# Blockwise inverses of triangular chunks: a quarter of the products moved to the diagonal tiles, and the side projections moved out

## The chip, the cores and the metric

One core of a Trainium2 chip. The metric is the device time of one execution in microseconds; three runs of the kernel before are shown, and one further execution was profiled.

## The reference, cut to what matters

All tensors are float32. A first block runs two layers; in each, an RWKV-7 branch steps a 64x64 state per head over 512 tokens. A second block has a gated delta net in both directions, whose chunk form needs an inverse of a unit lower triangular 64x64 matrix per chunk, head and direction:

```
state = state*w + (state @ -kk) (kk*a)^T + v k^T; y = state @ r      # RWKV, per token, 6 heads
x = x + concat(y_a, y_b, y_c) @ w_out[i]                             # 1024 x 1024, each layer
L = where(strict, (k*beta) @ k^T * decay, 0)                         # delta net, per chunk of 64
T = triangular_solve(eye + L, eye); u = T @ vb; w = T @ (kb*exp(gc))
gate_a, gate_d = split(sigmoid(h @ w_in[gate columns]))              # 2 x 1024 columns
merged = gate_a * (attn @ w_attn_up) + gate_d * (dn @ w_dn_up)
```

The kernel brings the RWKV recurrence into chunks of 64 tokens as well, with an inverse of the same kind.

## The kernel before, in words

Activations lie with channels on the 128 partitions and 512 tokens in columns. Two heads share a tile: partitions 0 to 63 and 64 to 127, the two halves. The program is a row of phases; in a phase each engine has its own instruction list, ordered by semaphores, and a phase ends with SP clearing the semaphores and a barrier.

**`invert` (line 914)** makes all inverses of a stage at once. A stage has groups of blocks, a block being one 64x64 matrix in each half. rwkv calls it once per layer (line 1282): 4 groups of 6 blocks, one direction. `delta_net` calls it once (line 2065): 8 groups of 8 blocks, four of each direction. The inverse is built by doubling: at level 0 the 2x2 blocks are written down, and each of the five levels 1 to 5 joins blocks of 2, 4, 8, 16 and 32. It keeps the inverse `inv` and its transpose `inv_t`. A job is one group at one level, so there are 5 x groups jobs (20 and 40). A job makes `half` = lower^T-product with `inv_t` in its step (banks 2 and 3 in turn), and two steps later the products for `inv` (banks 4 and 5) and `inv_t` (banks 6 and 7); step j on TensorE thus holds the first product of job j and the second ones of job j-2. At the last level `inv` isn't made.

TensorE works on quarters of its array, named by the half it reads and the half it writes. `half` and `inv_t` go across: read in one half, written to the other. `inv` stays within its half. The order in a step is, for every block, `half`, `inv`, `inv_t`, each for both halves (lines 987 to 996). Every float32 product shows as two matmul records and two weight loads. ScalarE copies `half` out of PSUM (line 1006, one instruction for all blocks), VectorE puts `inv` (1030) and `inv_t` (1031) under the level's mask with one predicated copy each and then lets `product_used` and `t_ready` go. TensorE's step j waits for `t_ready` of job j, `half_copied` of job j-2, and `product_used` of job j-4.

Level 0: SP moves `lower` into `inv` with the halves exchanged, two transfers per group (line 960), 96 KB each in rwkv and 128 KB in delta net. TensorE transposes `lower` by the identity (line 974, shown in the trace under line 967), VectorE copies it into `inv_t` (1019), then waits for the transfers of all groups, multiplies `inv` by the mask (1022) and adds the identity (1024), and goes to the next group.

**Side work in `invert`.** After each step TensorE does `portion` of a side projection: 128x512 products of 128x128 weight tiles (line 420), each tile gathered in bank 0 or 1. In rwkv these are output tiles 4 to 7 of `w_out` on the five k-tiles of attention rows that are ready (20 products in 22 steps), which VectorE adds to x (1217). In the delta net they are four tiles of the merge's gate columns, 8 products each (32 in 42 steps), which ScalarE copies (464) and SP spills to memory (453). Output tiles 0 to 3 of `w_out` are treated so in an earlier phase (`EARLY_OUT` = 4), ten of the gate tiles before the inverse (`BEFORE_INVERSE` = 10; `SPILLED` = 14 in all).

**After the inverse.** In rwkv a loop over the 8 chunks carries the state (1297 to 1326). Then `add_projection` (1418) takes k-tiles 0 to 2 of `w_out` for all eight output tiles: 3 products each, a ring of four weight tiles loaded by SP (1431), VectorE adding each to x (1451). `merge` (2157) makes the eight tiles of `merged`: 8 products for a tile whose two gates were spilled (m below `SPILLED // 2` = 7, gates read back on line 2177), else 24, with its 1.5 MB of weights, in a ring of two; step m's load is issued when tile m-2 is done.

Of the kernel before, what the change touches and what calls it, by code (L numbers as in the profile page):

```python
# [22 lines left out]
P = 128  # L23
# [26 lines left out]
def constant_parts():  # L50
# [44 lines left out]
    parts["strict"] = wide([c < r, c > r])  # L95
    parts["strict_T"] = wide([c > r, c < r])
# [34 lines left out]
def constant_offsets():  # L131
    at, where = 0, {}
    for n, a in constant_parts().items():
        where[n] = (at, a.shape[1])
        at += a.shape[1]
    where["neg_causal"] = (where["band"][0] + P, P)
    return where, at
# [776 lines left out]
def invert(nc, M, lower, inv, inv_t, groups, gsize, dirs, side, taker):  # L914
# [7 lines left out]
    def mask(lv, flip):  # L922

        return spread_out(level[:, lv, flip:flip + dirs, :].bitcast(U32))

    def ones(lv, flip):

        return spread_out(level[:, lv, flip:flip + dirs, :])

    def spread_out(m):  # L930

        if dirs == 1:
            return m.broadcast_to([P, blocks, CH])
        return m.unsqueeze(2).broadcast_to([P, dirs, blocks // dirs, CH])

# [7 lines left out]
    with ExitStack() as stack:  # L943
# [3 lines left out]
        with phase(nc, moved=0, eyes=0, lt_ready=0, t_ready=0, masked=0, inv_ready=0, half_copied=0, made=0, product_used=0, dve=0,  # L947
                   **side.SEMAPHORES) as (block, s):
            side.attach(s)
            steps = 5 * groups + 2  # L950
            portion = lambda step: side.products * step // steps

            halves = ((0, slice(0, HD)), (HD, slice(HD, P)))
            here_there = (halves, halves[::-1])

            @block.sync
            def _(sp):
                for g in range(groups):
                    for (_, here), (_, there) in zip(*here_there):
                        sp.dma_start(inv[there, g], lower[here, g]).then_inc(s["moved"], 16)  # L960
                side.load(sp)
                sp.wait_ge(s["moved"], 32 * groups)

            @block.tensor
            def _(pe):
# [3 lines left out]
                for g in range(groups):  # L969
                    if g >= 2:  # L970
                        pe.wait_ge(s["t_ready"], g - 1)
                    for b in range(blocks):
                        for row, here in halves:
                            last = mm(bank(4 + g % 2)[here, b, :], lower[here, g, b, :], M.c("ident2")[here, :], row, row)
                    last.then_inc(s["lt_ready"], 1)
                for job in range(steps):
                    g, k, old, og = job % groups, job % 2, job - 2, (job - 2) % groups
                    if job < 5 * groups:
                        pe.wait_ge(s["t_ready"], job + 1)
                    if old >= 0:  # L980
# [6 lines left out]
                    for b in range(blocks):  # L987
                        if job < 5 * groups:
# [1746 lines left out]
```

## Time and profile before

| | us |
|---|---|
| median of 3 runs | 2558.03 (2557.32 to 2561.3) |
| profiled execution, its own time | 2548.97 |
| its span in the trace | 2547.2 |
| TensorE matmul busy | 2242.9 (88%) |
| VectorE busy | 967.8 (38%) |
| ScalarE busy | 464.3 (18%) |
| mean granted TensorE clock | 0.944 of 2.4 GHz |

In the trace PE is TensorE's matmul side, PEld its weight loads, DVE VectorE, ACT ScalarE, SPq the queue of SP. A timeline line has start, length, engine, line, operation, output<-inputs, shape, count, and in brackets the idle time before it with what ended it. The first rwkv inverse lies at 412 to 476 us of the span, the second at 1036 to 1099, the delta net's at 1648 to 1796. The second layer repeats the first.

### The profile page before, as it was taken

Reading aid. Unit: us, or ns where it says so; the run is one execution under the profiler, and the core shown is the slowest. Engines: PE = TensorE matmul, PEld = TensorE weight load, DVE = VectorE, ACT = ScalarE, POOL = GpSimd, SP = SyncE. Lnnn points to the kernel's source line nnn. Section 1 sums busy time; section 2 is a strip of 40 time slices with the busy share of each in tenths; the row PEclk is TensorE's granted clock in tenths of the full one; section 3 lists DMA queues with packets and bytes.
Section 4 is the critical chain, followed back from the end, with each engine's and each line's share of the span. In section 5 each row is a group of like instructions: output and inputs, shape, how many; then the busy total and the mean of one; then the engine's idle time right before and its main releaser. Section 6 shows DMA issues by size and latency. Waiting matters only on the chain. (4 is left out here: it accounts for less than half of the span.)

```text
span 2547.2 us, 44008 instructions
## 1 busy us (share of the span) xinstructions
PE 2242.9 (88%) x18641; PEld 1169.4 (46%) x18641; DVE 967.8 (38%) x1768; ACT 464.3 (18%) x912; POOL 230.3 (9%) x181
## 2 busy tenths in 40 slices
PE   7989978879898998887898977879879979999998
PEld 3543436634363343763444533567644444444442
DVE  1157685332026767533233551454332251111112
ACT  1021431120102142111222332412110110000000
POOL 0111300000020310000004520400000000000000
PEclk9989999989998999998999988989989989999999
DMA  4134011021315300102101001110104549999997
GB/s 158 61 141 165 9 46 36 19 83 33 104 52 188 126 18 29 36 19 91 68 17 67 34 33 54 56 47 21 39 34 140 233 174 406 421 422 422 422 422 311
DMA packets 65238, 334.92 MB, mean 131 GB/s; under 512 B 7712, under 2 KB 11296, under 8 KB 36256
## 3 DMA queue, kind: packets, MB, share of 16 engines
q1 hardware_dynamic: 65056, 332.32, 34.2%
q8 instruction: 136, 2.23, 0.4%
q14 instruction: 46, 0.38, 0.0%
HBM read 322.06 MB, written 5.77 MB: 129 GB/s over the span
## 5 line engine op out<-in xcount | busy, mean ns | idle before, releaser
L420 PE MATMUL ps<-store,side_ring 128*128 128x512 f32 x784 | 396.6, 629 | 15.9 <-DMA side_ring<-in_w_rwkv 6.6
L2419 PE MATMUL ps<-expert_ring,xe 128*64 128x512 f32 x1024 | 223.2, 593 | 2.8 <-DVE back L2528 1.7
L420 PEld LDWEIGHTS ps<-store,side_ring 128*128 128x128 f32 x784 | 136.5, 194 | 171.2 <-issue 147.7
L333 PE MATMUL ps<-store,side_ring 128*128 128x512 f32 x384 | 168.2, 601 | 1.9 <-DVE store L299 1.9
L2419 PEld LDWEIGHTS ps<-expert_ring,xe 128*64 128x64 f32 x1024 | 73.0, 137 | 149.5 <-issue 147.4
L420 PE MATMUL ps<-store 128*128 128x512 f32 x224 | 115.2, 648 | 17.4 <-DMA store<-in_w_merge 16.8
L333 PEld LDWEIGHTS ps<-store,side_ring 128*128 128x128 f32 x384 | 74.0, 193 | 94.8 <-issue 92.3
L2447 PE MATMUL ps<-expert_ring,store 128*64 128x512 f32 x512 | 111.6, 594 | 1.4 <-DVE store L2504 1.4
L1504 PE MATMUL ps<-store,weight_ring 128*128 128x512 f32 x256 | 110.7, 593 | 1.9 <-DVE store L299 1.9
L2476 ACT ACTIVATE store<-ps 128x1024 f32<-128x1024 f32 x16 | 16.4, 1024 | 417.5 <-PE ps L2419 417.5
L509 POOL TENSOR_TENSOR attn_z<-attn_z,tables 128x512 f32<-128x512 f32 (+1 forms) x24 | 37.6, 1569 | 570.3 <-PE ps L498 568.2
L2491 DVE SCALAR_TENSOR_TENSOR x<-ps,mod,x 128x512 f32<-128x512 f32 x64 | 48.1, 751 | 108.0 <-PE ps L2396 103.6
L2189 PE MATMUL ps<-store,expert_ring 128*128 128x512 f32 x160 | 71.8, 611 | 11.2 <-DMA expert_ring<-in_w_merge 11.2
L1006 ACT ACTIVATE half<-ps 128x384 f32<-128x384 f32 (+1 forms) x80 | 43.5, 544 | 204.7 <-PE ps L967 204.7
L967 PE MATMUL ps<-inverses,matrices 64*64 64x64 f32 x1280 | 76.6, 220 | 2.9 <-DVE inverses L1024 2.1
L967 PE MATMUL ps<-half,inverses 64*64 64x64 f32 x1280 | 75.9, 218 | 2.5 <-issue 2.3
L1504 PEld LDWEIGHTS ps<-store,weight_ring 128*128 128x128 f32 x256 | 48.5, 190 | 62.5 <-issue 60.9
L575 DVE COPY attn_tok<-ps 128x456 f32<-128x456 f32 x8 | 5.1, 633 | 185.6 <-PE ps L565 185.6
L967 PEld LDWEIGHTS ps<-inverses,matrices 64*64 64x64 f32 x1280 | 63.9, 135 | 24.2 <-issue 21.1
L420 PEld LDWEIGHTS ps<-store 128*128 128x128 f32 x224 | 42.4, 203 | 65.6 <-issue 44.7
L1442 PE MATMUL ps<-store,weight_ring 128*128 128x512 f32 x96 | 45.8, 640 | 30.4 <-DMA weight_ring<-in_w_out 30.4
L2447 PEld LDWEIGHTS ps<-expert_ring,store 128*64 128x64 f32 x512 | 36.1, 137 | 71.0 <-issue 68.5
(426 smaller groups left out, 3838.2 us busy)
## 6 DMA issues: line engine op xcount, KB each, us to landing
expert_ring<-in_w_expert SPq DMA_DIRECT2D x192, 1024.0 KB, 16.4
mixed<-in_w_ada SPq DMA_DIRECT2D x24, 1024.0 KB, 4.8
side_ring<-in_w_attn SPq DMA_DIRECT2D x32, 512.0 KB, 3.7
side_ring<-in_w_rwkv SPq DMA_DIRECT2D x20, 512.0 KB, 4.4
weight_ring<-in_ple_gate SPq DMA_DIRECT2D x16, 512.0 KB, 4.2
store<-in_w_merge SPq DMA_DIRECT2D x14, 512.0 KB, 3.7
side_ring<-in_w_conv SPq DMA_DIRECT2D x12, 512.0 KB, 3.5
chosen<-in_w_o SPq DMA_DIRECT2D x8, 512.0 KB, 5.7
```

The costliest lines, as they stand in the source:

```text
L333: last = nc.tensor.matmul(ps[:, u, :], ring[:, u, k, :], src[:, k, :], start=(k == 0), stop=(k == kt - 1))
L420: ins = self.nc.tensor.matmul(self.ps[:, self.banks[j % banks], :], self.ring[:, j % self.slots, k, :], self.src[:, k, :], start=(k == 0), ...
L509: self.nc.gpsimd.tensor_tensor(self.z[rows, tile, :], self.z[rows, tile, :], self.M.table(f"cos_{table}")[rows], ALU.mult).then_inc(self.s ...
L967: return nc.tensor.matmul(out, lhs, rhs, start=True, stop=True, tile_position=(row, col))
L1006: nc.scalar.activation(half[:, job % 2], bank(2 + job % 2), ACT.Copy,).then_inc(s["half_copied"], 1)
L1442: last = nc.tensor.matmul(ps[:, j % 4, :], ring[:, j % 4, k, :], src[:, k, :], start=(k == 0), stop=(k == kt - 1))
L1504: last = nc.tensor.matmul(ps[:, j % 4, :], ring[:, j % 4, k, :], h[:, k, :], start=(k == 0), stop=(k == KT - 1))
L2189: last = nc.tensor.matmul(ps[:, 4 * (m % 2) + bank, :], ring[:, m % 2, k, :], src, start=(i == 0 or parts[i - 1][0] != bank), stop=(i == 2 ...
L2419: last = nc.tensor.matmul(ps[w, 2 * ep + half, :], xe[:, ep, k, :], ring[:, unit % SLOTS, k2, S * half:S * half + S], start=(k == 0), stop ...
L2447: last = nc.tensor.matmul(ps[w, 6 + half, :], act_t[:, ep, f, :], ring[:, units[ep] % SLOTS, f2, S * half:S * half + S], start=(f == 0), s ...
L2476: nc.scalar.activation(act_in[:, ep, :], ps[:, 2 * ep:2 * ep + 2, :].rearrange("p b n -> p (b n)"), ACT.Copy).then_inc(s["in_copied"], 1)
L2491: nc.vector.scalar_tensor_tensor(out=x[:, m, :], in0=ps[:, bank, :], scalar=gain(m), in1=x[:, m, :], op0=ALU.mult, op1=ALU.add).then_inc(s ...
```

## The change

- The side projection is taken out of `invert`. Output tiles 4 to 7 of `w_out` are then made whole (8 products) in `add_projection`; tiles 0 to 3 keep 3. `SPILLED` becomes 10, so four gate tiles are made in `merge`, where m = 5 and 6 now have 24 products.
- Of the blocks of each direction the first `width * 3 // 4` stay crossed (rwkv 4 of 6, delta net 3 of 4); the others go straight for `half` and `inv_t` too, and use banks 0 and 1 for both. The transfers of level 0 exchange the halves for crossed blocks alone, in four pieces per group for two.
- TensorE's order in a step alternates straight and crossed pairs. ScalarE has two copies per job and VectorE three.
- Level 0: the copies of `inv_t` go first for all groups; `inv` becomes one predicated copy of the identity per group, as its own transfers land.
- The constants lose `strict_T`, now a part of `strict`, and gain `not_first`.

```diff
-        with phase(nc, moved=0, eyes=0, lt_ready=0, t_ready=0, masked=0, inv_ready=0, half_copied=0, made=0, product_used=0, dve=0,
-                   **side.SEMAPHORES) as (block, s):
+        with phase(nc, moved=groups, eyes=0, lt_ready=0, t_ready=0, inv_ready=0, half_copied=0, made=0, straight_used=0, product_used=0, dve=0) as (block, s):
+            side = (slice(0, HD), slice(HD, P))
+            width = blocks // dirs
+            away = width * 3 // 4
+            crossed = [b for b in range(blocks) if b % width < away]
+            straight = [b for b in range(blocks) if b % width >= away]
...
+            def in_turn(within, across):
+                order, given = [], 0
+                for i, item in enumerate(within):
+                    upto = len(across) * (i + 1) // len(within)
+                    order += [(*item, 0)] + [(*other, 1) for other in across[given:upto]]
+                    given = upto
+                return order
...
                 for g in range(groups):
-                    for (_, here), (_, there) in zip(*here_there):
-                        sp.dma_start(inv[there, g], lower[here, g]).then_inc(s["moved"], 16)
-                side.load(sp)
-                sp.wait_ge(s["moved"], 32 * groups)
+                    for r in range(2):
+                        for cross in range(2):
+                            sp.dma_start(part(inv[side[r ^ cross], g], cross), part(lower[side[r], g], cross)).then_inc(s["moved"][g], 16)
+                for g in range(groups):
+                    sp.wait_ge(s["moved"][g], 64)
...
-                        pe.wait_ge(s["half_copied"], old + 1)
+                        pe.wait_ge(s["half_copied"], 2 * old + 2)
                     if old == 0:
                         pe.wait_ge(s["t_ready"], groups)
-                        pe.wait_ge(s["inv_ready"], groups)
+                    if 0 <= old < groups:
+                        pe.wait_ge(s["inv_ready"], old + 1)
                     if old >= 2:
                         pe.wait_ge(s["product_used"], old - 1)
...
+                    within = (of("inv_t", straight) if second else []) + \
+                        (of("inv", range(blocks)) if second and old < 4 * groups else []) + (of("half", straight) if first else [])
+                    across = (of("half", crossed) if first else []) + (of("inv_t", crossed) if second else [])
+                    for what, b, cross in in_turn(within, across):
...
+                            if what == "half":
+                                last = mm(bank(2 + k if cross else k)[side[c], at, :], lower[w, g, b, :], inv_t[w, g, b, :], HD * r, HD * c)
...
                     last.then_inc(s["made"], 1)
-                    side.multiply(pe, portion(job + 1))
...
-                    nc.scalar.activation(half[:, job % 2], bank(2 + job % 2), ACT.Copy,
-                                         ).then_inc(s["half_copied"], 1)
...
+                    nc.scalar.activation(part(half[:, job % 2], 1), part(bank(2 + job % 2), 1), ACT.Copy).then_inc(s["half_copied"], 1)
+                    if job >= 2:
+                        act.wait_ge(s["straight_used"], job - 1)
+                    nc.scalar.activation(part(half[:, job % 2], 0), slots(job % 2, 0), ACT.Copy).then_inc(s["half_copied"], 1)
...
-                    dve.wait_ge(s["moved"], 32 * groups)
-                    nc.vector.tensor_tensor(view(inv[:, g]), view(inv[:, g]), ones(0, 0), ALU.mult).then_inc(s["masked"], 1)
-                    dve.wait_ge(s["masked"], g + 1)
-                    nc.vector.tensor_tensor(inv[:, g], inv[:, g], eye, ALU.add).then_inc(s["inv_ready"], 1)
+                for g in range(groups):
+                    dve.wait_ge(s["moved"][g], 64)
+                    nc.vector.copy_predicated(inv[:, g], rest, eye).then_inc(s["inv_ready"], 1)
...
+                    nc.vector.copy_predicated(part(inv_t[:, g], 0), within, slots(k, 1)).then_inc(s["straight_used"], 1)
                     if lv < 5:
                         own.mark(nc.vector.copy_predicated(view(inv[:, g]), mask(lv, 0), view(bank(4 + k))))
-                    own.step(nc.vector.copy_predicated(view(inv_t[:, g]), mask(lv, 1), view(bank(6 + k))))
+                    own.step(nc.vector.copy_predicated(part(inv_t[:, g], 1), across, part(bank(6 + k), 1)))
+                    dve.wait_ge(s["straight_used"], job + 1)
                     dve.sem_inc(s["product_used"], 1)
                     dve.sem_inc(s["t_ready"], 1)
...
-BEFORE_INVERSE, SPILLED = 10, 14
+SPILLED = 10
...
-                    added = add_projection(nc, M, lambda j: w_out(j)[:, 0:RP, :], KT, RP, y[:, 0:RP, :], x)
+                    added = add_projection(nc, M, w_out, KT, KT, y, x, short=EARLY_OUT, part=RP)
```

`add_projection` takes `part` k-tiles for j below `short` and `kt` for the others, in its loads and its products.

## Rows read from the trace of the kernel before

**Rows 1.** Busy times by window: window, length, then each engine's; clock, DMA share, GB/s.

```profile
421.50:475.80 54.30, 53.13 (x1398) 36.50 (x1394) 25.48 (x47) 9.80 (x20) 0.00 (x0) 0.98 0.04 12
1677.90:1794.00 116.10, 111.72 (x3582) 85.21 (x3582) 48.83 (x72) 24.61 (x42) 0.00 (x0) 1.00 0.06 20
1648.10:1677.90 29.80, 15.53 (x322) 13.83 (x323) 16.26 (x24) 5.52 (x10) 0.00 (x0) 0.71 0.42 107
490.00:500.00 10.00, 7.55 (x210) 6.87 (x212) 3.33 (x10) 0.66 (x2) 0.00 (x0) 1.00 0.01 3
```

**Rows 2.** Timeline of ScalarE in the inverses, one copy per step.

```profile
450.62 0.49 ACT L1006 ACTIVATE half<-ps 128x384 f32<-128x384 f32 x1 [2.11 <-PE ps L967]
452.02 0.49 ACT L1006 ACTIVATE half<-ps 128x384 f32<-128x384 f32 x1 [0.91 <-PE ps L967]
...
1686.19 0.60 ACT L1006 ACTIVATE half<-ps 128x512 f32<-128x512 f32 x1 [2.47 <-PE ps L967]
1688.06 0.60 ACT L1006 ACTIVATE half<-ps 128x512 f32<-128x512 f32 x1 [1.27 <-PE ps L967]
1691.13 0.60 ACT L1006 ACTIVATE half<-ps 128x512 f32<-128x512 f32 x1 [2.47 <-PE ps L967]
...
1783.30 0.60 ACT L1006 ACTIVATE half<-ps 128x512 f32<-128x512 f32 x1 [2.47 <-PE ps L967]
1785.17 0.60 ACT L1006 ACTIVATE half<-ps 128x512 f32<-128x512 f32 x1 [1.27 <-PE ps L967]
```

**Rows 3.** Timeline inside one block: crossed `half,inverses`, straight `inverses,half`, both halves each.

```profile
1687.03 0.23 PE L967 MATMUL ps<-half,inverses 64*64 64x64 f32 x2
1687.04 0.14 PEld L967 LDWEIGHTS ps<-inverses,half 64*64 64x64 f32 x2
1687.04 0.27 PE L967 MATMUL ps<-inverses,half 64*64 64x64 f32 x2
```

**Rows 4.** Timeline of VectorE's copies and of the TensorE work they release.

```profile
413.32 0.59 DVE L1019 COPY_PREDICATED inv_t<-consts,ps 128x384 f32<-128x384 uint32 x1 [1.81 <-PE ps L967]
414.02 0.20 PEld L967 LDWEIGHTS ps<-consts,raw 64*64 64x64 f32 x4 [0.26 <-DVEq L1020]
...
428.15 0.14 PEld L967 LDWEIGHTS ps<-inv_t,raw 64*64 64x64 f32 x2 [0.76 <-issue]
...
429.82 0.59 DVE L1030 COPY_PREDICATED inv<-consts,ps 128x384 f32<-128x384 uint32 x1 [1.56 <-PE ps L967]
430.30 0.57 DVE L1031 COPY_PREDICATED inv_t<-consts,ps 128x384 f32<-128x384 uint32 x1
...
1680.05 0.73 DVE L1030 COPY_PREDICATED inverses<-consts,ps 128x512 f32<-128x512 uint32 x1 [2.27 <-PE ps L967]
1680.67 0.71 DVE L1031 COPY_PREDICATED inverses<-consts,ps 128x512 f32<-128x512 uint32 x1
```

**Rows 5.** Timeline of SP's transfers of level 0, and VectorE's first use.

```profile
412.24 5.00 SPq L960 DMA_DIRECT2D inv<-raw  x8
418.88 0.56 DVE L1022 TENSOR_TENSOR inv<-inv,consts 128x384 f32<-128x384 f32 x1 [4.97 <-DMA inv<-raw]
...
1648.16 11.02 SPq L960 DMA_DIRECT2D inverses<-matrices  x16
```

**Rows 6.** Timeline of VectorE: the first instruction of the phase after each inverse.

```profile
477.35 0.22 DVE L1337 MEMSET state<- 128x192 f32 x1 [1.58 <-PEq L209]
...
1798.08 0.48 DVE L2123 MEMSET inverses<- 128x512 f32 x1 [4.85 <-PEq L209]
```

**Rows 7.** Two tiles of the projection on VectorE; chain of waits in the merge.

```profile
547.88 0.69 DVE L1451 TENSOR_TENSOR x<-ps,x 128x512 f32<-128x512 f32 x1 [12.57 <-PE ps L1442]
550.46 0.69 DVE L1451 TENSOR_TENSOR x<-ps,x 128x512 f32<-128x512 f32 x1 [1.88 <-PE ps L1442]
...
1943.79 7.02 DMA expert_ring<-in_w_merge
...
1950.86 20.87 PE ps L2189 x48
```

More of the change, by code:

```diff
@@ L136, in constant_offsets @@
     where["neg_causal"] = (where["band"][0] + P, P)
+    where["strict_T"] = (where["strict"][0] + CH, 2 * CH)
+    where["strict"] = (where["strict"][0], 2 * CH)
     return where, at
@@ L911, in attention_branches, with invert @@
                   M.tables.rearrange("p (u h) n -> p u h n", u=2))
-def invert(nc, M, lower, inv, inv_t, groups, gsize, dirs, side, taker):
+def invert(nc, M, lower, inv, inv_t, groups, gsize, dirs):
     ps = M.ps
@@ L922, in mask @@
     def mask(lv, flip):
[L924 to L930, printed above, removed]
+        m = level[:, lv, flip:flip + dirs, :].bitcast(U32)
         if dirs == 1:
@@ L972, in _ @@
                     for b in range(blocks):
-                        for row, here in halves:
-                            last = mm(bank(4 + g % 2)[here, b, :], lower[here, g, b, :], M.c("ident2")[here, :], row, row)
+                        for r in range(2):
+                            last = mm(bank(4 + g % 2)[side[r], b, :], lower[side[r], g, b, :], M.c("ident2")[side[r], :], HD * r, HD * r)
                     last.then_inc(s["lt_ready"], 1)
@@ new lines, in _ @@
+                    across = (of("half", crossed) if first else []) + (of("inv_t", crossed) if second else [])
+                    for what, b, cross in in_turn(within, across):
+                        at = b if cross or what == "inv" else straight.index(b) + (len(straight) if what == "inv_t" else 0)
+                        for r in range(2):
+                            c, w = r ^ cross, side[r]
+                            if what == "half":
+                                last = mm(bank(2 + k if cross else k)[side[c], at, :], lower[w, g, b, :], inv_t[w, g, b, :], HD * r, HD * c)
+                            elif what == "inv":
+                                last = mm(bank(4 + k)[w, at, :], half[w, k, b, :], inv[w, og, b, :], HD * r, HD * r)
+                            else:
+                                last = mm(bank(6 + k if cross else k)[side[c], at, :], inv[w, og, b, :], half[w, k, b, :], HD * r, HD * c)
@@ L1279, in rwkv_branch @@
             pairs_of = lambda a: a[:, :, :, :].rearrange("p (g c) j t -> p g (c j) t", c=2)
-            out_ring = sbt("side_ring", [P, 3, KT - RP, P])
-            side = SideProjection(nc, M, [add(j) for j in range(EARLY_OUT, KT)], KT - RP, y[:, RP:KT, :], out_ring, 3, (0, 1))
-            invert(nc, M, pairs_of(low), pairs_of(inv), pairs_of(inv_t), NCH // 2, 2 * RP, 1, side, "vector")
+            invert(nc, M, pairs_of(low), pairs_of(inv), pairs_of(inv_t), NCH // 2, 2 * RP, 1)
             state, xs, sa = sbt("state", [P, 2, RP, HD]), sbt("xs", [P, 2, RP, CH]), sbt("sa", [P, 2, RP, CH])
@@ L1415, in _, with add_projection @@
                     own.step(nc.vector.tensor_tensor(yr, yr, z[:, R_G:R_G + 3, :], ALU.mult))
-def add_projection(nc, M, weights, n, kt, src, x, gain=None, ready=None, free=1, ring=None):
+def add_projection(nc, M, weights, n, kt, src, x, gain=None, ready=None, free=1, ring=None, short=0, part=0):
     ps = M.ps
@@ L1438, in _ @@
                         pe.wait_ge(s["added"], j - 3)
-                    for k in range(kt):
+                    use = part if j < short else kt
+                    for k in range(use):
                         if ready and j == 0:
```

50 lines of the change are left out of this document (20 added, 30 removed).

## The prediction

> **What bounds the kernel now.** I read busy time and granted clock by stage first, because the page's totals mix stages with different limits, and then the timelines engine by engine. In the two kinds of inverse stage TensorE has the full clock (2.4 GHz) and is busy all the time, while VectorE and ScalarE are busy less than half of it [rows 1]. From one of ScalarE's copies to the next is one step of the pipeline: 1.87 us in delta net and 1.40 in rwkv for a step without a side product, 3.07 with one [rows 2]. So a side product costs 1.20 us there, more than its 0.86 in a row of its kind (part 5): nothing of it lies beside the small blocks.
>
> What is in 1.87 us? Eight blocks, each with two pairs of products across the halves (`half`, `inv_t`) and one pair within them (`inv`): 16 crossed pairs and 8 straight ones. At the last level `inv` is not made, so 16 crossed pairs alone, and the step is again 1.87, from 1783.30 to 1785.17 [rows 2]. So the crossed pairs set it, at 0.117 us each, and the straight ones are free beside them. rwkv says the same: 12 crossed pairs x 0.117 = 1.40. Inside a block, straight weight loads and matmuls start within 20 ns of crossed ones [rows 3].
>
> **The change, part by part.**
>
> 1. *Balance.* rwkv (6 blocks, 4 stay crossed): crossed 2x4 = 8 pairs, straight 2x2+6 = 10, so TensorE's work in a step, W, is 10 x 0.117 = 1.17 us for 1.40. Delta (8 blocks, 6 crossed): 12 and 12, W = 1.40 for 1.87. Last level: rwkv 0.94, delta 1.40. That both directions can be kept full no step of before shows; the bounds are these values and no gain (1.40 and 1.87). I take the full gain, since in rows 3 crossed and straight matmuls run side by side and the crossed ones, by rows 2, lose nothing by it. The Trainium skill (TensorE: Matmul & The Clock Gate, Part 3, The mechanism) says that a weight load overlaps matmuls in flight only where the row group differs; straight and crossed products of one half share it, so by that rule the balance gives nothing, which is rival A. The trace disagrees: the load at 1687.04 starts behind matmuls on both halves that started at 1687.03.
>
> 2. *What comes after W.* Step j starts when VectorE has taken job j-4, made in step j-2, for the banks are used in turn. From a step's start to VectorE's start is 429.82 - 428.15 = 1.67 us: W 1.40 and 0.27. From VectorE's end (413.91) to TensorE's start is 0.11 [rows 4]; with one more semaphore wait I take 0.14. VectorE now has three instructions for two. Start to start 384 columns are 0.48 and 512 are 0.62 [rows 4], so 128 add 0.14 and the straight part (128 columns) takes some 0.21; the last instruction counts with its whole length. rwkv: 0.21 + 0.48 + 0.44 = 1.13. Delta: 0.21 + 0.62 + 0.58 = 1.41. Two steps take W + 0.27 + this + 0.14: rwkv 2.71, a step 1.355; delta 3.22, a step 1.61. So the return through VectorE sets the step, and part of the balance is lost. The 128-column copy stands in no row: bounds 0.08, the part that doesn't grow with columns, and 0.48, as for 384; that is -0.07 to +0.14 us a step. ScalarE's two copies end before VectorE's three (its one copy of 384 columns takes 0.49, rows 2), and the `straight_used` it waits for comes from the first of these.
>
> 3. *Level 0.* All `inv_t` copies go first now, and the `inv` ones follow each landing, so steps 0 to 3 run under the transfers. But VectorE does every group's `inv` before job 0, and step 4 waits for job 0: step 4 hangs on the last transfer. SP issues 16 transfers for 8 in rwkv, at 5.00/8 = 0.625 us, and 32 for 16 in delta, at 11.02/16 = 0.69; the last of the eight started at 416.6 and VectorE at 418.88 [rows 5], 2.3 us. The bytes are the same. rwkv: 412.24 + 15 x 0.625 + 2.3 = 423.9, a copy 0.5, job 0 with its signal 1.3: step 4 at 425.8. Before: step 3 at 428.15, and 2.60 (1.40 + 1.20) later step 4, 430.75. Delta: 1648.16 + 31 x 0.69 + 2.4 = 1672.0, + 0.7 + 1.6: 1674.3, against 1684.1 before (VectorE took job 0 at 1680.05, so step 2 began at 1677.9; two steps of 3.07). TensorE idles ahead of step 4 and may restart at the lower clock (0.71 was granted in delta's level 0 [rows 1]); I add 1.5 us to each stage. What an issue of a split piece costs no row shows: bounds 0.625 and double 0.69.
>
> 4. *A stage.* rwkv: 425.8 + 1.5 + 14 x 1.355 = 446.3 at step 18; steps 18 to 21, without `inv`, and VectorE's last copy 4.7; the next phase's memset another 1.6 later [rows 6]: 452.6 for 477.35, **-24.8** a layer. Delta: 1674.3 + 1.5 + 30 x 1.605 = 1724.0 at step 34; six steps at 1.40 or a little more, two short ones and the last copy 11.5; 1.5 for stalls of TensorE's own that rows 2 leave out and that stay; 1.6 to the memset: 1738.6 for 1798.08 [rows 6], **-59.5**. In this 38.4 is 32 side products x 1.20, and some 3 is the last side tile's spill, which the end of the phase waited for.
>
> 5. *The side work comes back.* rwkv: four tiles of 5 products go to the projection that follows, which is TensorE's alone: three products in 550.46 - 547.88 = 2.58, 0.858 each [rows 7]. 20 x 0.858 = **+17.2** a layer. Tiles 4 to 7 load 320 KB more each, issued on SP when the tile four earlier is done; three tiles (7.7 us) cover that. Delta: the gates of m = 5 and 6 are made in the merge, 2 x 16 products at 0.86 (24 in 20.87 [rows 7]): **+27.5**. Tile 5 now loads 1.5 MB as tile 7 did, 7.02 us from issue [rows 7]; the issue comes as tile 4 starts, 8 x 0.86 = 6.9: +0.3. Adds and spills that go lay beside TensorE: 0. SP has 16 issues more in delta, and nothing is queued behind them now that the side loads are gone. The constants keep their size.
>
> Sum: -2 x 24.8 - 59.5 + 2 x 17.2 + 27.5 + 0.3 = **-46.9 us**. That is against the profiled execution, 2548.97 (span 2547.2 and 1.8 around it): 2502. The median of the runs shown is 9 us above it; I give the forecast against the median, 2558 - 47 = **2511**.
>
> **Rivals.** A: *the balance gives nothing*; the four tiles can't be kept full (dispatch, or weight loads). W stays 1.40 and 1.87: rwkv's step is (1.40 + 1.54)/2 = 1.47, delta's 1.87. 14 x 0.115 + 1.0 = 2.6, twice, and 30 x 0.265 + 3.1 = 11.1: +16, **2527**. For it: no whole step of before issues more than 24 pairs in 1.87 us, and this asks for 24 in 1.40. Against: rows 3.
>
> B, *the other side*: without side products TensorE idles a little in each step, and the clock is granted at 1.2 GHz through the loops. A pair is then 0.234: rwkv's step 2.34 (+16.6 a layer), delta's 2.81 (+46): +79, **2590**. It decides from 47/79 = 60% of the loops at the lower clock. Against: the state loop had the full clock with TensorE busy 7.55 of 10 us [rows 1], and ours is busy 1.17 of 1.355.
>
> C: *a split piece costs double at issue.* Step 4 comes 22 us later in delta and 10 in each rwkv: +42, **2553**. Against: an issue cost nearly the same for 96 KB and 128 KB, rwkv's and delta's [rows 5].
>
> **How the numbers follow.** Forecast 0.66, A 0.22, C 0.05, B 0.05, no net effect for a reason I don't see 0.02. The forecast's own range is 2504 to 2519, by the clock allowances (4.5 down), the 128-column copy (3 down, 7 up) and the stalls. With A inside and 5 us for the level of the runs (the profiled one lies 9 lower) the range is 2498 to 2534. About 0.2%, 5 us, is what a measurement of this kernel can tell. Faster 0.93, same 0.03, slower 0.04.
>
> **What would show it.** ScalarE's copies 1.35 and 1.6 us apart; 1.87 in delta is A. Delta's last level at 1.40 tests the balance alone. TensorE's loads waiting for VectorE. The memset at 452.6; the delta stage 59 us shorter. The projection 17 us longer, the merge 27. A granted clock of 0.5 in the loops is B; an issue of SP over 1 us is C. The forecast is wrong if the three stages together gain less than the 62 us that the moved work costs.

## The result, and the profile after

The changed kernel takes **2567.1 us**, the kernel before 2556.2 beside it on the same chip: ratio **1.0041**, 95% interval [1.0028, 1.0054]. It is slower by 0.4%; 2511 was forecast, below every run. The profiled executions span 2565.4 and 2547.2 us, so their difference, 18.2, is larger than that of the medians (11), because the profiled execution of before, 2548.97, lies 7 us under this median. What follows compares the two profiles.

Timeline of SP and VectorE after the change, the rows that answer to [rows 5] and [rows 6] (start, length, in brackets the idle time before and what ended it):

```profile
412.98 11.64 SPq L979 DMA_DIRECT2D inv<-raw  x16
...
426.10 0.58 DVE L1044 COPY_PREDICATED inv<-consts 128x384 f32<-128x384 uint32 x1 [1.44 <-DMA inv<-raw]
...
464.52 0.22 DVE L1354 MEMSET state<- 128x192 f32 x1 [1.63 <-PEq L211]
...
1662.93 23.98 SPq L979 DMA_DIRECT2D inverses<-matrices  x32
...
1688.56 0.73 DVE L1044 COPY_PREDICATED inverses<-consts 128x512 f32<-128x512 uint32 x1 [1.88 <-DMA inverses<-matrices]
1689.18 0.28 DVE L1050 COPY_PREDICATED inverses<-consts,ps 128x128 f32<-128x128 uint32 x1
1689.37 0.72 DVE L1052 COPY_PREDICATED inverses<-consts,ps 128x512 f32<-128x512 uint32 x1
1689.98 0.56 DVE L1053 COPY_PREDICATED inverses<-consts,ps 128x384 f32<-128x384 uint32 x1
...
1790.52 0.48 DVE L2142 MEMSET inverses<- 128x512 f32 x1 [1.92 <-PEq L211]
```

From the first transfer to the next phase's memset, rwkv's stage is 464.52 - 412.98 = 51.5 us where it was 477.35 - 412.24 = 65.1: 13.6 shorter (13.8 in the second layer), not 24.8. Delta's is 127.6 for 149.9: 22.3 shorter, not 59.5. So 49.7 us were gained, where 109.1 were forecast, and less than the 62 that the prediction named as its sign of being wrong.

The moved work cost what was forecast. The rows that answer to [rows 7], of VectorE and of the chain of waits:

```profile
539.82 0.69 DVE L1470 TENSOR_TENSOR x<-ps,x 128x512 f32<-128x512 f32 x1 [1.89 <-PE ps L1461]
542.39 0.69 DVE L1470 TENSOR_TENSOR x<-ps,x 128x512 f32<-128x512 f32 x1 [1.89 <-PE ps L1461]
...
1927.96 62.07 PE ps L2208 x144
```

Three products still take 2.57, and the projection, first to last matmul, went from 21.7 to 40.0 and from 22.9 to 39.8 us: +18.3 and +16.9 (17.2 each was forecast). From delta's memset to the end is 749.1 before and 774.8 after, +25.8 (27.8). The rest, some 7 us, is scattered over the stretches between and belongs to no part of the change that I can name. -49.7 + 61.0 + 7 = +18.

Level 0 isn't where the miss is, either. VectorE's first job ends at 427.7 and 1690.5, 14.7 and 27.6 us after the first transfer; the forecast had step 4 start 15.1 and 27.6 after it, allowances included. All of the miss lies behind step 4: 464.5 - 427.8 = 36.7 us in rwkv (25.3 forecast) and 99.9 in delta (62.8), together 60 us.

**What the loops look like.** Windows of the full steps, from ScalarE's copy of step 3 to its last of level 4 (12 steps in rwkv, 28 in delta; columns as in [rows 1]); first the kernel before, then the one after:

```profile
429.81:459.82 30.01, 30.01 (x887) 20.93 (x888) 14.01 (x26) 5.88 (x12) 0.00 (x0) 1.00 0.05 15
1053.48:1083.49 30.01, 30.01 (x887) 20.93 (x888) 14.00 (x26) 5.88 (x12) 0.00 (x0) 1.00 0.05 15
1683.12:1766.10 82.98, 79.11 (x2731) 60.91 (x2732) 37.63 (x57) 17.70 (x31) 0.00 (x0) 1.00 0.08 23
```

```profile
427.08:452.68 25.60, 18.09 (x882) 16.77 (x885) 13.88 (x39) 7.60 (x26) 0.00 (x0) 0.92 0.02 4
1058.95:1083.87 24.92, 18.08 (x882) 16.63 (x885) 13.90 (x38) 7.57 (x25) 0.00 (x0) 0.93 0.02 4
1689.67:1768.27 78.60, 48.88 (x2709) 45.53 (x2713) 39.88 (x86) 19.20 (x57) 0.00 (x0) 0.95 0.02 4
```

Delta's full step went from 82.98/28 = 2.96 us, a side product included in most, to 78.60/28 = 2.81 with none. TensorE is busy 62% of the time and VectorE 51%: something else holds the step. It shows in TensorE's timeline, as idle time in the middle of a step that no wait explains ("issue" in the brackets: the engine waited for nothing that the profile shows):

```profile
1718.60 0.27 PE L986 MATMUL ps<-inverses,matrices 64*64 64x64 f32 x1 [1.45 <-issue]
1722.47 0.27 PE L986 MATMUL ps<-inverses,matrices 64*64 64x64 f32 x2 [1.78 <-issue]
1726.38 0.27 PE L986 MATMUL ps<-half,inverses 64*64 64x64 f32 x2 [1.82 <-issue]
```

The gaps come 3.9 us apart. Between them TensorE's instructions can be counted (matmuls and weight loads, windows that begin just before each gap ends):

```profile
1718.58:1722.45 3.87, 2.09 (x127) 1.96 (x128) 1.38 (x3) 0.66 (x2) 0.00 (x0) 1.00 0.01 4
1722.45:1726.36 3.91, 2.09 (x128) 1.95 (x127) 1.40 (x3) 0.66 (x2) 0.00 (x0) 1.00 0.01 4
1726.36:1730.21 3.85, 2.41 (x127) 2.16 (x127) 2.78 (x6) 1.43 (x4) 0.00 (x0) 1.00 0.02 4
```

That is 254 or 255 each time. A count over single records, with the one or two semaphore instructions of TensorE's sequencer that the windows leave out, gives exactly 256 from gap to gap. Here it is with the instruction packets of the DMA view beside it (times in us):

```
gap 1720.69 -> 1722.47, 256 instructions since the last gap
   packet of 16 KB 1724.16 -> 1725.08
gap 1724.56 -> 1726.38, 256 instructions since the last gap
   packet of 16 KB 1727.86 -> 1728.95
gap 1729.07 -> 1730.23, 256 instructions since the last gap
   packet of 16 KB 1731.78 -> 1732.74
gap 1732.32 -> 1734.15, 256 instructions since the last gap
```

The DMA view over 1720 to 1760, in 40 slices of 1 us, shows nothing but these packets:

```profile
GB/s 16 0 0 0 16 0 0 16 0 0 0 16 0 0 0 16 0 0 0 16 0 0 16 0 0 0 16 0 0 0 16 0 0 0 16 0 0 16 0 0
```

The same count over other loops: in side_moved (below) the 21 gaps of over 0.5 us in delta's full steps all lie 256 instructions apart, and in the kernel before the only four such gaps there lie 256, 768 and 2560 apart, whole packets too.

**The theory this gives (supply).** TensorE's instructions arrive in packets of 256 (16 KB / 256 = 64 B each). TensorE starts on one; 1.5 to 1.7 us later the next packet is on its way, takes 0.9 to 1.1, and 1.3 to 1.4 later its instructions run. Over the row of slices above the packets come 3.7 us apart; the theory puts it as one packet each 3.75 us, 68 instructions a microsecond, whatever the tiles could do. The Trainium skill (Runtime: NRT & Kernel Launch, Instruction fetch mechanics) describes such a sequence, blocks of 256 instructions that the engine's sequencer fetches a page ahead through a DMA queue of its own; the counts agree. It adds that the fetch hides behind the engine's slower issue. Here it doesn't: these 256 instructions are 2.1 us of work.

A full step of delta is 48 products of four instructions (two loads, two matmuls), 192: 2.82 us of supply. rwkv's is 144: 2.12. The forecast asked for 192 in 1.605 us, 120 a microsecond. The kernel before already ran delta's full steps at (2731 + 2732)/82.98 = 66. A side product is 0.86 to 1.20 us of work in *four* instructions.

### The profile page after: what moved, and what is told of

The parts are those of the page before. It is cut to its first block and busy times, and to the rows that moved or that the text cites. A ratio compares the mean times of both kernels' runs of the same rounds, so it can differ in the third digit from the quotient of the medians.

```text
span 2565.4 us, 44140 instructions
## 1 busy us (share of the span) xinstructions
PE 2211.3 (86%) x18641; PEld 1155.0 (45%) x18641; DVE 957.5 (37%) x1824; ACT 470.3 (18%) x988; POOL 230.2 (9%) x181
## 5 line engine op out<-in xcount | busy, mean ns | idle before, releaser
L422 PE MATMUL ps<-store,side_ring 128*128 128x512 f32 x704 | 352.0, 627 | 14.5 <-DMA side_ring<-in_w_rwkv 6.5
L422 PEld LDWEIGHTS ps<-store,side_ring 128*128 128x128 f32 x704 | 124.6, 195 | 167.1 <-issue 147.8
L335 PE MATMUL ps<-store,side_ring 128*128 128x512 f32 x384 | 168.2, 601 | 1.9 <-DVE store L301 1.9
L335 PEld LDWEIGHTS ps<-store,side_ring 128*128 128x128 f32 x384 | 74.0, 193 | 95.0 <-issue 92.4
L1523 PE MATMUL ps<-store,weight_ring 128*128 128x512 f32 x256 | 110.7, 593 | 1.9 <-DVE store L301 1.9
L1461 PE MATMUL ps<-store,weight_ring 128*128 128x512 f32 x176 | 81.0, 624 | 32.5 <-DMA weight_ring<-in_w_out 32.5
L2208 PE MATMUL ps<-store,expert_ring 128*128 128x512 f32 x224 | 98.8, 603 | 11.3 <-DMA expert_ring<-in_w_merge 11.2
L422 PE MATMUL ps<-store 128*128 128x512 f32 x160 | 80.0, 655 | 17.6 <-DMA store<-in_w_merge 17.1
L1523 PEld LDWEIGHTS ps<-store,weight_ring 128*128 128x128 f32 x256 | 48.5, 190 | 62.5 <-issue 60.9
L2208 PEld LDWEIGHTS ps<-store,expert_ring 128*128 128x128 f32 x224 | 43.2, 194 | 67.7 <-issue 54.0
L986 PE MATMUL ps<-half,inverses 64*64 64x64 f32 x1280 | 50.8, 226 | 26.5 <-issue 13.2
L1461 PEld LDWEIGHTS ps<-store,weight_ring 128*128 128x128 f32 x176 | 35.1, 201 | 78.3 <-issue 44.2
L986 PE MATMUL ps<-half,inv 64*64 64x64 f32 x960 | 44.5, 235 | 25.4 <-DVEq L1056 12.8
L2523 DVE TENSOR_TENSOR store<-ps,store 128x512 f32<-128x512 f32 x16 | 11.1, 692 | 147.4 <-ACT store L2501 147.4
```

The source lines that it names most:

```text
L335: last = nc.tensor.matmul(ps[:, u, :], ring[:, u, k, :], src[:, k, :], start=(k == 0), stop=(k == kt - 1))
L422: ins = self.nc.tensor.matmul(self.ps[:, self.banks[j % banks], :], self.ring[:, j % self.slots, k, :], self.src[:, k, :], start=(k == 0), ...
L986: return nc.tensor.matmul(out, lhs, rhs, start=True, stop=True, tile_position=(row, col))
L1461: last = nc.tensor.matmul(ps[:, j % 4, :], ring[:, j % 4, k, :], src[:, k, :], start=(k == 0), stop=(k == use - 1))
L1523: last = nc.tensor.matmul(ps[:, j % 4, :], ring[:, j % 4, k, :], h[:, k, :], start=(k == 0), stop=(k == KT - 1))
L2208: last = nc.tensor.matmul(ps[:, 4 * (m % 2) + bank, :], ring[:, m % 2, k, :], src, start=(i == 0 or parts[i - 1][0] != bank), stop=(i == 2 ...
```

## The experiments

The rivals of the supply theory: the chain through VectorE and the new `straight_used` wait; tiles that can't be kept full; and the prediction's own view, in which only tile work and VectorE count.

**side_moved.** The kernel before; of the change only the side products' move:

```diff
-            side = SideProjection(nc, M, [add(j) for j in range(EARLY_OUT, KT)], KT - RP, ...
+            side = SideProjection(nc, M, [], KT - RP, ...
-            ... beside(BEFORE_INVERSE, SPILLED, (0, 1)), "scalar")
+            ... SideProjection(nc, M, [], KT, h, room, 2, (0, 1)), "scalar")
-BEFORE_INVERSE, SPILLED = 10, 14
+SPILLED = 10
```

and `add_projection` as in the change.

> The kernel before with its own inverse (five products of a block as they were, two transfers per group, all of level 0 as it was), but with the side products moved out of it as the change moves them. Supply theory: in the loops TensorE gets its instructions 256 at a time, one packet each 3.75 us (68 a microsecond), whatever the tiles could do. A full step of delta is 192 instructions, 2.8 us; one of rwkv 144, 2.1 us. Delta's stage gets some 12 us shorter (138 for 150), rwkv's 10 each (55 for 65), and the 62 us of moved work come back: about +30, ratio 1.012. Theory of the prediction (crossed pairs at 0.117 us set the step): steps of 1.40 and 1.87 us, the stages 24 and 41 us shorter, -27 in all, ratio 0.989. If the four tiles' balance in the change is at fault (bank or tile conflicts), this kernel has nothing of it and follows the second.

Measured: ratio **1.0122** [1.0101, 1.0143]; stages 52.9, 53.5 and 135.4 us. Its windows of the full steps:

```profile
430.33:455.64 25.31, 19.34 (x878) 18.16 (x882) 12.71 (x25) 5.91 (x13) 0.00 (x0) 1.00 0.02 4
1702.30:1781.59 79.29, 57.30 (x2699) 54.48 (x2696) 37.59 (x56) 16.73 (x28) 0.00 (x0) 1.00 0.02 5
```

25.31/12 = 2.11 and 79.29/28 = 2.83 us a step, as the supply theory says, with work of 1.40 and 1.87. With the old tiles, the old VectorE copies and no new wait, the loops last as long as in the changed kernel (25.6, 24.9; 78.6). So the balance brought nothing there, and none of the change's new waits is to blame. The changed kernel's stages are 1.4, 2.2 and 7.8 us shorter than these, nearly all of it ahead of the windows: level 0.

ScalarE's copies in this kernel's rwkv loop lie 1.40 and 2.77 us apart:

```profile
432.41 0.49 ACT L1006 ACTIVATE half<-ps 128x384 f32<-128x384 f32 x1 [1.59 <-PE ps L967]
433.81 0.49 ACT L1006 ACTIVATE half<-ps 128x384 f32<-128x384 f32 x1 [0.91 <-PE ps L967]
436.58 0.49 ACT L1006 ACTIVATE half<-ps 128x384 f32<-128x384 f32 x1 [2.27 <-PE ps L967]
```

One step runs at its tile work, the next has a gap of the supply in it. 1.40 or 1.87 seen singly is therefore no proof that a loop can keep it up.

**no_inv.** The changed kernel without the products that renew `inv`; VectorE's copies stay:

```diff
-                        (of("inv", range(blocks)) if second and old < 4 * groups else []) + (of("half", straight) if first else [])
+                        [] + (of("half", straight) if first else [])
```

> The changed kernel without the `inv` products of levels 1 to 4 (that part of the inverse is left out, VectorE's copies stay, from what lies in the bank). Supply theory: 64 instructions of 192 fewer in a delta step, 48 of 144 in rwkv, so steps of 1.9 and 1.4 us; 2048/68 = 30 us less in delta and 11 in each rwkv, about -52 against the changed kernel, ratio to the kernel before 0.984. Rival, the return through VectorE and the straight_used wait: no product of it is gone, the ratio stays 1.004. Rival, the tiles can't be kept full: fewer straight products leave the crossed ones, which set the step; also near 1.004.

One run: 2525.4 us, 0.988 of before (0.984 expected). Its windows:

```profile
428.72:447.29 18.57, 15.85 (x576) 14.44 (x576) 13.72 (x38) 7.69 (x25) 0.00 (x0) 0.85 0.02 4
1675.43:1730.11 54.68, 47.26 (x1792) 44.10 (x1792) 39.98 (x86) 19.84 (x58) 0.00 (x0) 0.96 0.02 4
```

Delta's step: 54.68/28 = 1.95 us for 1.88 by supply and 2.81 with the products. The chain through VectorE kept all its copies and waits, so it wasn't what held the step. In rwkv 18.57/12 = 1.55 for 1.41, and there the steps between two gaps are 1.38 apart, with TensorE waiting for VectorE before each:

```profile
437.47 0.27 PE L986 MATMUL ps<-half,inv 64*64 64x64 f32 x2 [0.21 <-DVEq L1056]
437.50 0.30 DVE L1050 COPY_PREDICATED inv_t<-consts,ps 128x128 f32<-128x128 uint32 x1 [0.27 <-PE ps L986]
...
438.19 0.43 DVE L1053 COPY_PREDICATED inv_t<-consts,ps 128x256 f32<-128x256 uint32 x1
...
438.85 0.27 PE L986 MATMUL ps<-half,inv 64*64 64x64 f32 x2 [0.22 <-DVEq L1056]
438.88 0.30 DVE L1050 COPY_PREDICATED inv_t<-consts,ps 128x128 f32<-128x128 uint32 x1 [0.27 <-PE ps L986]
```

That is the return of part 2. It exists, below the supply's bound: from VectorE's first copy (437.50) to its last one's end 1.12 us (1.13 forecast), 0.23 more to TensorE's start (0.14 forecast), and from there 1.41 to VectorE's next start at 440.26, 2.76 for two steps. That the step comes so near the forecast's 1.355 is partly luck: by part 2's own terms the work left in this kernel, eight crossed pairs, would be 0.94 and two steps 2.48. 1.41 less 0.27 leaves 1.14; why its 12 pairs took that long no run shows.

**padded.** The changed kernel with tiny products at the head of each step:

```diff
+                    for i in range(2 * blocks * 3 // 4 if second else 0):
+                        r = i % 2
+                        nc.tensor.matmul(ps[side[r], k, 256 + i:257 + i], lower[side[r], g, 0, :], M.c("ident2")[side[r], 0:1],
+                                         start=True, stop=True, tile_position=(HD * r, HD * r))
```

> The changed kernel with tiny products added at the head of each step (one moving column each, to unused columns of the straight bank): 12 a step in delta and 9 in rwkv, four instructions each, 48 and 36. Supply theory: 1920/68 = 28 us more in delta and 11 more in each rwkv, +50, ratio to before 1.024. Rivals (VectorE's return, waits): TensorE has 30 to 40% idle in each step and takes them there; ratio stays near 1.004. Tiles: one column of work, under 0.4 us a step at most, of which the idle time takes most: under +10 us, 1.008.

One run: 2633.5 us, 1.031. Windows:

```profile
428.67:468.25 39.58, 38.74 (x1089) 38.75 (x1090) 13.83 (x38) 7.39 (x25) 0.00 (x0) 0.50 0.02 4
1730.51:1828.82 98.31, 73.45 (x3372) 70.82 (x3372) 40.00 (x86) 18.55 (x57) 0.00 (x0) 0.88 0.02 4
```

Delta's step is 98.31/28 = 3.51 us; 240 instructions at 68 are 3.53. Its stage is 26.9 us longer than the changed kernel's; 28 was expected. rwkv missed: +19.0 and +17.4 for 11. The reason stands in its row: a granted clock of 0.50, 1.2 GHz, over the whole window, with TensorE busy 38.7 of 39.6 us. That loop was held by work at half clock, not by supply: its steps are all 3.20 us. The clock is rival B's, though not by its reason, for TensorE wasn't idle. Delta had part of it too: 0.50 was granted from 1730.5 to 1744 and from 1754.3 to 1761.1 us. Over the 19 steps from 1764.57 to 1828.82, at a mean clock of 0.97, a step takes 3.38 us, 0.57 more than the changed kernel's 2.81. Nor are the tiny products without work. 3.20 less ten pairs at 0.234 leaves 0.86 for nine of them at the lower clock, so an estimate for delta's twelve at the higher one is 0.57 us a step.

**long_products.** The counterpart: as much work as a side product, in eight instructions:

```diff
+                    for i in range(2 if second else 0):
+                        nc.tensor.matmul(ps[:, k, 256:512], lower[:, g, 0:2, :].rearrange("p b t -> p (b t)"), M.c("level")[:, 0:256],
+                                         start=True, stop=True)
```

> The changed kernel with two long products at the head of each step (128x128 by 256 columns, to unused columns of the straight bank): as much tile work as one side product, 1.20 us in these loops, in eight instructions. It is the counterpart of the tiny products: much work, few instructions. Supply theory: a delta step has 1.40 + 1.20 = 2.6 us of work and 200 instructions, 2.9 us of supply, so it hides: +5 us in delta; in rwkv 1.17 + 1.20 = 2.37 is over the supply (152 instructions, 2.2 us), so 20 steps come to 47 us for 37 to 39, +8 each; +21 in all, ratio to before 1.012. If a step were held by tile work, or by TensorE's own work and then VectorE's return in a chain, all of it would be added: 80 steps x 1.2 = +96, ratio 1.042.

One run: 2597.8 us, 1.016. Windows, and three of ScalarE's first copies in rwkv:

```profile
427.84:458.86 31.02, 30.18 (x913) 24.36 (x914) 13.90 (x39) 7.44 (x26) 0.00 (x0) 0.94 0.02 4
1704.20:1790.90 86.70, 79.39 (x2801) 64.40 (x2801) 40.03 (x86) 18.54 (x57) 0.00 (x0) 0.97 0.02 4
```

```profile
432.76 0.39 ACT L1032 ACTIVATE half<-ps 128x256 f32<-128x256 f32 x1 [3.44 <-PE ps L986]
...
435.13 0.38 ACT L1032 ACTIVATE half<-ps 128x256 f32<-128x256 f32 x1 [1.75 <-PE ps L986]
...
437.50 0.38 ACT L1032 ACTIVATE half<-ps 128x256 f32<-128x256 f32 x1 [1.76 <-PE ps L986]
```

28 x 1.20 = 33.6 us of work in delta's full steps made them 8.1 longer (86.70 for 78.60). So padded and long_products together: 48 instructions with some 0.57 us of work (the estimate above) cost 0.70 us a step, or 0.57 where the clock was nearly full; eight with 1.20 us of work cost 0.29. Twice the work in a sixth of the instructions cost about half: that separates supply from work. The stages grew by 12.9 in delta (5 expected, for in the last level, with 128 instructions a step, the work sets the pace at 2.62) and by 8.5 each in rwkv (8).

It also settles rival A. rwkv's step is 435.13 - 432.76 = 2.37 = 1.17 + 1.20, and delta's in the last level 2.62, against 1.40 + 1.20. rwkv's last level has 2.15 = 0.94 + 1.20, so from 8 to 10 to 12 pairs the step grows by 0.11 to 0.13 a pair, whatever the long products themselves cost:

```profile
465.72 0.38 ACT L1032 ACTIVATE half<-ps 128x256 f32<-128x256 f32 x1 [1.50 <-PE ps L986]
...
467.87 0.38 ACT L1032 ACTIVATE half<-ps 128x256 f32<-128x256 f32 x1 [1.54 <-PE ps L986]
```

The changed kernel shows it as well: four of delta's steps in the last level take 1.40 us (ScalarE's copies at 1776.24 and 1777.64, for one), where the kernel before had 1.87 [rows 2]. With something to fill the supply's gaps, **the balance gives all that part 1 said**.

**level0_alone.** The kernel before with two transfers per group and a count per group, and this:

```diff
-                    dve.wait_ge(s["moved"], 32 * groups)
-                    nc.vector.tensor_tensor(view(inv[:, g]), view(inv[:, g]), ones(0, 0), ALU.mult).then_inc(s["masked"], 1)
-                    dve.wait_ge(s["masked"], g + 1)
-                    nc.vector.tensor_tensor(inv[:, g], inv[:, g], eye, ALU.add).then_inc(s["inv_ready"], 1)
+                for g in range(groups):
+                    dve.wait_ge(s["moved"][g], 32)
+                    nc.vector.copy_predicated(inv[:, g], rest, eye).then_inc(s["inv_ready"], 1)
```

> The kernel before with only the first level changed: all inv_t copies first, then one predicated copy for inv per group as that group's own two transfers land. Side products stay where they were. Both theories: step 4 comes some 7 us earlier in rwkv (transfers are 8 issues, not 16; the side tile's load then limits) and 15 in delta, and the loops after it keep their pace, so about -29 us, ratio 0.989. If the loops are held by the supply of instructions counted from the stage's start and not by their own pace, half of it is given back: 0.995.

Measured: **0.9962** [0.9949, 0.9975]; stages 65.4, 64.8 and 138.3. Delta gave 11.6 us, rwkv nothing. TensorE's timeline in rwkv's step 1 says why:

```profile
423.74 2.07 PE L422 MATMUL ps<-store,side_ring 128*128 128x512 f32 x2 [4.88 <-DMA side_ring<-in_w_out]
```

The first side product waits for its tile, which SP issues behind the eight transfers, and the steps queued behind it wait too. I had expected this load to leave 7 us of the gain; it left none. The ratio lies near the 0.995 of the expectation's other theory, a supply counted from the stage's start; the next run decides between the two.

**level0_late_side.** The same, and one line:

```diff
-            portion = lambda step: side.products * step // steps
+            portion = lambda step: side.products * max(step - 4, 0) // (steps - 4)
```

> The first level alone, as before (ratio 0.996: in rwkv TensorE stood still for 4.9 us in step 1, for the side products' first tile, whose load is queued behind the eight transfers), now with no side product before step 4; the same number is spread over the steps from 4 on. If that wait was what gave the gain back: rwkv's stages 3 us shorter than before, delta's 13 us, -19 in all, ratio 0.9925. If the gain was lost because TensorE's work in the stage is the limit anyway, nothing changes: 0.996.

Measured: **0.9909** [0.9887, 0.9931]; stages 59.9, 63.3 and 136.5. It was that wait. The second layer's stage is 3.4 us longer than the first's; its full steps had a mean granted clock of 0.91 for 1.00.

**one_straight_bank.** The balance on top of it, with the side work kept. The side products need a bank, so the straight products of both parities share one, and TensorE waits in mid-step for last step's copies from it:

```diff
+                            if 1 <= job <= 5 * groups:
+                                pe.wait_ge(s["half_copied"], 2 * job)
+                            if job >= 3:
+                                pe.wait_ge(s["straight_used"], job - 2)
...
-            ... out_ring, 3, (0, 1))
+            ... out_ring, 3, (1,))
+                    for r in range(2):
+                        sp.dma_start(part(inv[rows[1 - r], g], 1), part(lower[rows[r], g], 1)).then_inc(s["moved"][g], 16)
+                    nc.scalar.activation(part(inv[:, g], 0), part(lower[:, g], 0), ACT.Copy).then_inc(s["eyes"], 1)
```

> The same level 0 and late side products, with the change's balance over the four tiles and the side work kept inside: the straight products of both parities share one bank (TensorE waits in the middle of a step for last step's copies from it), the side products use the other. The straight blocks' level-0 part is copied by ScalarE, so only two transfers per group are left. Supply theory: delta 6800 instructions at 68 a microsecond, 100 us from step 4, stage 124 us (149.9 before); rwkv 18 x 1.17 + 20 x 1.20 = 45 us of work, over its supply of 40, stage 60 (65.1): -36, ratio 0.986. Tile theory without a limit of supply: delta 38 x 1.40 + 38.4 = 92, stage 116, ratio 0.983. If the wait in mid-step holds TensorE, 0.4 us a step, 58 steps: ratio 0.995.

Measured: **0.9862** [0.9837, 0.9887], 2522.6 us for 2557.0: faster than both kernels. Stages 56.7, 56.4 and 133.0; windows:

```profile
424.42:454.64 30.22, 28.69 (x889) 18.92 (x890) 14.67 (x39) 7.36 (x25) 0.00 (x0) 1.00 0.09 30
1655.78:1740.71 84.93, 72.71 (x2733) 52.29 (x2734) 39.14 (x85) 19.80 (x59) 0.00 (x0) 0.98 0.08 23
```

The total came as expected, its parts didn't quite: rwkv better by 3.5 each, delta 9 worse. Its full steps take 3.03 us, not 2.88: 64 instructions a microsecond. level0_late_side's, with the old tiles, take 2.96 in the row below, so in these steps the balance gained nothing; in rwkv it brought 2.60 down to 2.37. I read delta's steps as supply and work adding up in part where they are nearly equal: the 12 gaps of over 0.5 us there still lie whole packets apart, but no run separates the two. And its last eight steps take 2.64, about the work of a step with a side product in it; side_by_supply, below, has 2.6 there without one.

```profile
1667.48:1750.25 82.77, 80.76 (x2731) 61.75 (x2726) 37.63 (x56) 17.70 (x30) 0.00 (x0) 0.99 0.08 23
```

**side_by_supply.** An attempt to go further: side products where the supply leaves room.

```diff
-            portion = lambda step: side.products * max(step - 4, 0) // (steps - 4)
+            portion = lambda step: min(max(step - 4, 0) + (step > 14) + (step > 18), side.products) if dirs == 2 else \
+                min(2 * (max(step - 2, 0) // 2), side.products)
```

> The kernel of one_straight_bank with the side products placed by what limits each step. Delta: one in each full step from 4 on (192 instructions, supply 2.8 us, work 1.40 + 1.20) and none in the last eight (128 instructions, supply 1.9). Supply theory: the full steps stay as long, since they have slack, and the last eight go from 2.62 to 1.9 us, -6; the last side tile's spill no longer ends the phase, -2; stage 125 us for 133.0. rwkv: two products together after every second step; if the 1.20 us is 0.86 of work and 0.34 for the change between small blocks and whole tiles, ten changes fewer save 3.4 us each, stage 53 for 56.5. -15 in all, ratio 0.981. If the full steps have no slack, delta's stage stays at 131 to 133 (the same work, in another place); if pairs in rwkv open holes in the return through VectorE, its stage stays at 56: ratio 0.986.

Measured: **0.9908** [0.9890, 0.9926], slower than the kernel it starts from; stages 58.7, 62.9 and 136.2. Both halves of the expectation fell. Delta's last eight steps stayed at 2.6 us without any side work, by the added wait for last step's copies, which the side products had covered (without `inv` the straight products come first, so it stands at the step's head); two of VectorE's copies and the matmul that waited:

```profile
1762.62 0.30 DVE L1075 COPY_PREDICATED inverses<-consts,ps 128x128 f32<-128x128 uint32 x1 [1.20 <-PE ps L995]
1763.54 0.27 PE L995 MATMUL ps<-half,inverses 64*64 64x64 f32 x2 [0.96 <-DVEq L1080]
1765.21 0.30 DVE L1075 COPY_PREDICATED inverses<-consts,ps 128x128 f32<-128x128 uint32 x1 [1.81 <-PE ps L995]
```

And the full steps, with one side product in each, came to 91.63/28 = 3.27 us; they had no slack. In rwkv a pair saves nothing. The step between two pairs has no side product to cover the same wait: TensorE's load stands in mid-step until ScalarE has copied last step's straight part (line 1052):

```profile
438.57 0.30 DVE L1075 COPY_PREDICATED inv_t<-consts,ps 128x128 f32<-128x128 uint32 x1 [0.97 <-PE ps L995]
441.83 0.31 DVE L1075 COPY_PREDICATED inv_t<-consts,ps 128x128 f32<-128x128 uint32 x1 [2.17 <-PE ps L995]
442.50 0.32 PEld L995 LDWEIGHTS ps<-half,inv 64*64 64x64 f32 x16 [0.19 <-ACT half L1052]
443.27 0.30 DVE L1075 COPY_PREDICATED inv_t<-consts,ps 128x128 f32<-128x128 uint32 x1 [0.32 <-PE ps L995]
```

From one first copy of VectorE's to the next, 1.44 and 3.26 are 4.70 for two steps, where even spreading has 2 x 2.37 = 4.74. A pair that crosses from one output tile to the next also waits for the single side bank to be emptied; I take two steps of 4.70 and 4.44 us in the first layer (3.26 otherwise) for that, which wasn't tried by itself.

## Why the prediction was wrong

- **Part 1, balance**: W right (1.17 and 1.40, by the steps of 2.37 and 2.62 in long_products), but W was not the bound. Rival A fell, and with it, for these loops, the rule on loads of one row group that part 1 cites from the Trainium skill (TensorE: Matmul & The Clock Gate, Part 3, The mechanism): these steps leave no room for it.
- **Part 2, the return through VectorE**: its terms right (from one copy's start to the next 0.19, then 0.61, and 0.56 for the last, in rows 1689.18 to 1689.98; 1.36 for the 1.41 summed; in rwkv 1.12 for 1.13), but for TensorE's start behind VectorE, 0.23 us for 0.14 in no_inv. With W at 1.17 the measured terms give 1.395 a step, an estimate, for 1.355. But "the return through VectorE sets the step" was wrong. The supply did.
- **Part 3, level 0**: right within 0.5 us, in part by luck. An issue of a split piece cost 11.64/16 = 0.73 and 23.98/32 = 0.75, 0.10 and 0.06 more than before, so rival C fell; but VectorE took the last group 13.1 and 25.6 us after the first transfer, for 11.7 and 23.8 summed, and the allowance of 1.5 us, meant for the clock, paid for that. The lower clock still held behind step 4's start (0.50 from 427 to 431 us and from 1690 to 1694).
- **Part 4 is the step that failed.** "14 x 1.355", "30 x 1.605" and "In this 38.4 is 32 side products x 1.20" price a step at its tile work and the return, and take the side products out at their full length. The runs show 2.12 and 2.81 a step with or without the balance: a side product's length was mostly time in which the next packet came. The sum lost 60 us here. The miss of the forecast, 2567 - 2511 = 56, is that; the 7 us of scattered time and the 9 that the forecast added for the level of the runs nearly cancel.
- The hint stood in "1.5 for stalls of TensorE's own". I took steps of 3.4 to 3.9 us in delta for accidents that cost a fixed sum. The four gaps of 0.58 to 1.24 us in mid-step there, whole packets apart, were this limit, touched now and then; without side products it is met in nearly every packet.
- And it could be computed from [rows 1]: (3582 + 3582)/116.1 = 62 instructions a microsecond in delta, 51 in rwkv. The forecast asked for 120, nearly twice what any loop shown had kept up. The step of 1.87 without a side product, 103 a microsecond, only ever stood alone, between steps with one.
- **Part 5** was right: +35.2 for 34.4 in the projections and +25.8 for 27.8 in the rest of the kernel behind delta's stage.
- **Rival B** fell for this change: the granted clock is 0.92 to 0.95 over the full steps and 1.00 in the rows from 1718 to 1730. side_moved's rwkv loops, at 1.00, last as long. No rival named the supply. The last one, "no net effect for a reason I don't see", had 0.02.

## What to carry to other kernels

In a loop of small products, count instructions per microsecond beside busy time: an engine that is shown busy, at full clock, may be near the rate at which its instructions arrive, and then a product costs its instructions, not its work. Long products laid between small ones are nearly free there, and taking them out gains little while they cost their full length elsewhere; keep them and shorten the work around them, as one_straight_bank does; that paid in rwkv and in the last levels, and not where the steps already ran near the supply. A stall that no wait explains, in the middle of a run of instructions, should be counted from one to the next before it is called noise.

## What the runs showed of the hardware

- TensorE's instructions come 256 at a time; in the changed kernel's full steps of delta they take 3.4 to 4.1 us from the start of one packet's work to the next's, 3.75 in the mean. Rates over full steps: 68 to 71 a microsecond where the work is short (the changed kernel, side_moved; padded in delta), 64 to 66 where it comes near (the kernel before, one_straight_bank and long_products, all in delta).
- In padded's rwkv loops, in both layers, TensorE was busy 38.74 of 39.58 us and the granted clock stayed at 0.50 (1.2 GHz). The changed kernel, which differs by the tiny products alone, had 0.92 and 0.93 there.
- No more than one packet came ahead, even in idle time: before delta's step 4 the changed kernel's TensorE stood still from 1679.93 to 1690.75 us. One packet landed at 1681.29, and the next set out at 1693.51, when TensorE was at work again.
- Why instructions run only 1.3 us after their packet has landed stays open; no run tried it.
